# Slots of the late token tiles placed anew in a fused decoder step

## The reference

```python
def layer(x, c, ...):
    mod = jax.nn.silu(c) @ w_mod + b_mod
    sh1, sc1, g1, sh2, sc2, g2 = jnp.split(mod, N_MOD, axis=-1)
    m, st = token_mixers(modulate(x, sh1, sc1), w_in, ..., w_out, conv_buf, s0, past)
    x = x + g1[:, None, :] * m
    x = x + g2[:, None, :] * peer(modulate(x, sh2, sc2), peer_wq, peer_subkeys, peer_u, peer_v)
    return x, st
```

```python
    act = jax.nn.gelu(jnp.einsum('thkd,td->thk', pu[eidx], xb), approximate=False) * gate
    return jnp.einsum('thk,kd->td', act, pv[eidx])
```

## Time and profile before

| | us |
|---|---|
| median of three runs | 2171.68 (2168.19 to 2176.35) |
| the profiled execution | 2157.73 |
| its span | 2155.9 |
| TensorE busy | 1614.1 |
| VectorE busy | 1442.2 |
| GpSimd busy | 873.9 |
| ScalarE busy | 491.2 |

### The profile page before, as it was taken

The page is one execution under the profiler, slowest core; times in us unless marked ns, Lnnn a source line. Parts: engine busy times, 40 slices in busy tenths (PEclk is TensorE's granted clock), DMA queues, the critical chain, the costliest instruction groups (busy, mean ns, idle before and its releaser), DMA issues.

```text
span 2155.9 us, 25076 instructions
## 1 busy us (share of the span) xinstructions
PE 1614.1 (75%) x8048; PEld 856.8 (40%) x8048; DVE 1442.2 (67%) x3392; ACT 491.2 (23%) x1348; POOL 873.9 (41%) x646
## 2 busy tenths in 40 slices
PE   6999978878876766767576666667786777777776
PEld 4545547546663432343243233334322432221222
DVE  4246766555369976667998666799867668664754
ACT  2112213111132222223222122323212222221221
POOL 0286770312016643334564333456333334443442
PEclk9999999888988987898899889879898988898999
DMA  8487647977668999999899999989999999999996
GB/s 287 125 264 249 225 128 237 313 228 229 225 258 322 377 418 414 411 414 384 313 381 414 415 415 410 388 328 387 410 388 392 414 389 365 400 413 385 420 397 276
DMA packets 169989, 733.39 MB, mean 340 GB/s; under 512 B 17757, under 2 KB 18606, under 8 KB 103154
## 3 DMA queue, kind: packets, MB, share of 16 engines
q0 software_dynamic: 75024, 545.82, 63.1%
q1 hardware_dynamic: 94834, 185.96, 25.0%
HBM read 722.69 MB, written 9.12 MB: 339 GB/s over the span
## 4 chain that ended last, share of the span: by engine, by line
DMA 34%; PE 33%; DVE 18%; issue 5%; POOL 4%; SPq 3%; ACT 3%; DVEq 0%; ACTq 0%; POOLq 0%
PE bank L474 32%; DMA RING<-in_peer_uv,R 19%; DMA R<-in_peer_uv,R 11%; DVE RING L2078 6%; DVE R L2078 2%; SPq L2347 2%; ACT R L1330 2%; POOL RING L2327 2%; DMA R<-in_w_out 1%; SPq L2406 1%; DMA R<-h2s_d 1%; PE bank L481 1%; POOL R L2327 1%; DVE R L1881 1%; POOL R L2307 1%
## 5 line engine op out<-in xcount | busy, mean ns | idle before, releaser
L474 PE MATMUL bank<-RING,R 128*64 128x512 f32 (+2 forms) x1560 | 542.3, 695 | 287.6 <-ACT R L1330 276.3
L2327 POOL DMA_INDIRECT RING<-in_peer_uv,R x390 | 448.6, 1150 | 727.3 <-PE bank L474 595.8
L474 PE MATMUL bank<-R 128*128 128x128 f32 (+6 forms) x2216 | 408.8, 389 | 145.0 <-ACT R L1330 131.9
L2078 DVE SCALAR_TENSOR_TENSOR RING<-RING,MV 128x1024 f32<-128x1024 f32 x288 | 362.9, 1260 | 189.4 <-DMA RING<-in_peer_uv,R 182.2
L474 PEld LDWEIGHTS bank<-RING,R 128*64 128x64 f32 (+2 forms) x1560 | 165.7, 165 | 565.6 <-issue 549.3
L474 PEld LDWEIGHTS bank<-R 128*128 128x128 f32 (+3 forms) x2216 | 255.7, 187 | 321.2 <-issue 315.6
L1319 ACT ACTIVATE R<-R 128x2 f32<-128x2 f32 x256 | 52.1, 203 | 1099.8 <-DVE RING L2078 892.9
L2327 POOL DMA_INDIRECT R<-in_peer_uv,R x130 | 145.6, 1120 | 218.7 <-PE bank L474 200.5
L2078 DVE SCALAR_TENSOR_TENSOR R<-R,MV 128x1024 f32<-128x1024 f32 x96 | 126.4, 1316 | 82.9 <-DMA R<-in_peer_uv,R 82.1
L2078 DVE SCALAR_TENSOR_TENSOR RING<-RING,R 128x1024 f32<-128x1024 f32 x96 | 125.3, 1305 | 56.3 <-DMA RING<-in_peer_uv,R 51.9
L474 PEld LDWEIGHTS bank<-HT,R 128*128 128x128 f32 x1024 | 123.4, 196 | 47.0 <-issue 45.8
(11 more groups left out here) (320 smaller groups left out, 1765.4 us busy)
## 6 DMA issues: line engine op xcount, KB each, us to landing
R<-in_peer_wq SPq DMA_DIRECT2D x16, 2048.0 KB, 28.0
RING<-in_w_mod SPq DMA_DIRECT2D x12, 2048.0 KB, 8.1
MV<-in_cache_k SPq DMA_DIRECT2D x88, 256.0 KB, 3.8
R<-in_cache_v SPq DMA_DIRECT2D x84, 256.0 KB, 3.6
R<-in_w_out SPq DMA_DIRECT2D x6, 2048.0 KB, 32.9
MV<-in_cache_v SPq DMA_DIRECT2D x44, 256.0 KB, 3.7
RING<-in_w_in SPq DMA_DIRECT2D x5, 2048.0 KB, 9.5
R<-in_cache_k SPq DMA_DIRECT2D x40, 256.0 KB, 3.7
```

Of the source, the lines that this page charges most:

```text
L474: i = nc.tensor.matmul(out, lhsT, rhs, start=start, stop=stop, **k)
L2078: V.scalar_tensor_tensor(u, u, 1.0, H2HIGH if s_ % 2 and n < PAIRED * PH else H2[n // PH % 2], ALU.mult, ALU.mult, accum_out=DOT[:, n % 4, ...
L2327: nc.gpsimd.indirect_dma_start(UV[g % UN], None, a["peer_uv"][0], bass.IndirectOffsetOnAxis(ap=idx, axis=0)).then_inc(S(f"uv_in{g % UN}"), 16)
```

## The change

It changes at which event a slot stands. The order of the slots of a tile stays, and no instruction is added or removed.

```diff
-            slots = post_slots(tile)
-            at = max(len(delta_slots()), 112 - slots.index(("wq", 3, 0, 0)))
-            begin = delta_slots() if tile >= LATE else []
-            assert len(begin) <= at and at + len(slots) <= PH * STEPS
-            for first, some in ((0, begin), (at, slots)):
-                for x, s_ in enumerate(some):
-                    slots_at.setdefault((tile - 1) * PH * STEPS + first + x, []).append((tile,) + s_)
+            at = 0
+            for x, s_ in enumerate(delta_slots()):
+                at = x * 5 // 4 if tile < TILES - 1 else x
+                slots_at.setdefault((tile - 1) * PH * STEPS + at, []).append((tile,) + s_)
+            together = 0
+            for s_ in post_slots(tile):
+                together = together + 1 if s_[0] == "wq" else 0
+                at += together % 2 if together else 1
+                slots_at.setdefault((tile - 1) * PH * STEPS + at, []).append((tile,) + s_)
+            assert at < PH * STEPS
```

## The result

| | us |
|---|---|
| before, median of 20 runs | 2169.82 (2155.77 to 2180.34) |
| after, median of 20 runs | 2187.49 (2171.59 to 2208.26) |
| ratio, 95% interval | 1.0072 (1.0047 to 1.0098) |
| profiled execution after | 2175.94 |

The change makes the kernel slower by 0.7%. The medians lie 17.7 us apart; the ratio leaves out executions in a second, slower state of the chip, here the one of 2208.26 us. The forecast was 2171 us and no change, with 2187 as its upper end.

The account below looks back on a forecast made before the run. No engine alone bounds it; time can be won only where DMA runs under 415 GB/s. Terms - 7.0 + 6.0 + 0.5 = - 0.5 us gave 2157.2 profiled, 2171 us as median; range 2163 to 2180, with the terms' ends 2158 to 2187.

Parts of the forecast that it names:

- Two query slots to an event: Query slots behind value pairs: packing them wins nothing and costs 0.5 us in tile 3, ends 0 and 4.
- It fits: Four query slots behind a value pair take TensorE 6.0 us for two events, against 6.5 us the DMA needs.
- wq 2 and wq 3 0 to 3 us late, covered: Third and fourth query weights in tiles 1 and 2: 0 to 3 us late, covered by gathers taking 11.3 us to land.
- rival 1: Slower, 2190 us (+ 18 us): TensorE's waits for weights at slots 74 and 78, then wq 2 and 3; chance 0.19.
- The delta rule over 75 events: Tiles 1 and 2: spreading 60 delta slots relieves VectorE, 3.5 us gained per tile, together 7 us, ends 0 and 18.
- The output weights: w_out in tiles 1 and 2: later issue makes TensorE wait 4.4 then 9 us, costing 3 us per tile, ends 0 and 8.
- Rival 2: Delta units of VectorE: the relief works in full, 18 us won, 4 paid, - 14 us, 2157 us; chance 0.21.
- The tile's opening pile: Sums, residual, gate scaling, decays and products in the second tile's first delta unit: 9.6 of 12.8 us lost, stays.
- the signs of being wrong: Waits for wq over 5 us; pile shrunk over 2 us; a full-rate unit longer without weights moved into it.

Follow-up runs that it names:

- delta_only: Against the kernel before: delta rule over 75 events in tiles 1 and 2 as in the change, query slots still one to an event; 0.9989, 2163.39 us.
- after_spaced: The change with its query groups 10 events apart instead of 6; 1.0005 of the kernel before, 2173.05 us.
- pair_only: Against the kernel before: query slots two to an event in all three tiles, delta slots and first output slot left as before; 1.0102.
- pair_again: pair_only measured once more, word for word; 1.0085 of the kernel before.
- pair_beside: pair_only with seven eighths of each late query weight transfer sent to unread scratch, unwaited; 1.0019 of before, 1.0056 over the kernel before with the same split.
- the halved kernels: pair_beside and its base, the kernel before with the same split, each with half the late query matmuls left out; 1.0005 and 1.0017 of before.
- pair_act_late: pair_only with ScalarE's copy of each query block one event later; 1.0066 of the kernel before.
- tile3_old: The change with tile 3 left as before it; 1.0038 of the kernel before.

## Why the prediction was wrong, by its own steps

**Two query slots to an event: the step that failed.** It said "It fits" and counted 0.5 us, for tile 3 alone, with 4 as the upper end. Measured, the packing with its groups 6 events apart costs 1.0072 / 0.9989 against delta_only, 0.8% or 18 us, and 1.0072 / 1.0005 against after_spaced, 0.7% or 15 us; each has an interval of some 0.4% to each side. The duration was right (3.84 us for four slots). Two things were wrong:
- The steps were followed as if only w_out could hold TensorE for long, with "wq 2 and wq 3 0 to 3 us late, covered". In the trace there are five waits for `in_peer_wq`, 15.2 us together, up to 5.83. Behind the two of them that lasted 3.31 and 5.83 us in tiles 1 and 2, four slots took 5.23 and 5.68 instead of 3.84 us, at a granted clock of 0.72 over the first and of 0.50, the lower of the two levels, in the first 2 us of the second; behind two waits of under 1 us they took 3.84. Groups of 6 events at 3.25 us give 20 us, a transfer in the queue needs 23 or more. That arithmetic stood in rival 1 and should have been in the sum. In pair_only and pair_again the cover is used up in the unit of events 96 to 111, where the waits and the emptied queue stand together; in tiles 1 and 2 of the change's own profile the waits are there and the queue stays full.
- "Fits" compared TensorE's 6.0 us with 6.5 us for two events and left 0.5. The groups need more room than that: at 8 events to a group there is no wait for query weights and still 0.5% of loss, and pair_beside has 0.6% over its base without them. Which link in the loop of buffer, dot product, gelu, diagonal and value sum carries it is open. TensorE's own work is a candidate, but the halved kernels do not show it, as there the base slowed down and not the packed kernel sped up. ScalarE's in-order waits at the query copies (68.9 us against 22.6) are another; pair_act_late did not settle it.

**The delta rule over 75 events: 7 us of gain forecast, ends 0 and 18; none seen.** delta_only gives this and the w_out term together - 0.1%, - 2.4 us with an interval from - 8 to + 3; the forecast for the two was - 1. The sum agrees, but partly by luck: its two terms were not seen apart, and in the traces neither came out as forecast. In the traces the first two units win 2.1 us (18.6 to 16.5), less than the 4.0 forecast, while the third and fourth lose 6.7 more, not 0.5. The third unit was costed by VectorE's busy time staying under the floor (38.60 us it is, under 40.4), and it lost 5.1 us all the same. So busy time under the floor did not make a unit run at the floor where masks and corrections stand in it. And the fourth unit of before, with weights in flight, ran at 413 GB/s; with the delta tail moved in and the weights moved out it ran at 391, and in tile3_old, with the same slots, at 408. By this measure the four units together lose 4.6 us more than before and not 3.5 less; why delta_only is no slower for it is open.

**The output weights: 3 us a tile, ends 0 and 8.** The first wait came as forecast (4.4; 4.85 and 3.91 us in tiles 1 and 2). The second, 9 us, did not come: the longest w_out transfer took 41.3 us from issue to landing and held a weight load up for 0.8 us, where the longest of before took 50.4. The Trainium skill, "DMA: Bandwidth & Descriptors", section "Queues, rings and completion order", has the engines take turns between rings that have work; by it weights go faster as soon as TensorE's first wait thins out the gathers. The trace agrees, and that of before did so already: of tile 3's two transfers the first took 27.40 us and the median of both was 32.7, so the second some 38. In tiles 1 and 2 of before, where TensorE did not wait, the second took 50. I took 50, from there.

**Rivals.** Rival 1 (waits win, 2190, chance 0.19) had the sign and the size, 2190 against 2187. Its own condition, TensorE over 5 us at least three times a tile, was not met: in the trace two waits for weights last over 5 us in all, 5.83 and 7.82, and tile 3 had the like of the second before. Of its places, slots 74 and 78 cost nothing measurable, and how much wq 2 and 3 cost by their waits alone is not shown. So that it hit the number is in part luck. That the packed groups cost without waits stood in no rival. Rival 2 did not happen. The tile's opening pile moved by one event and lost 11.8 instead of 12.8 us, as said. Of the signs of being wrong two came: a wait for wq over 5 us, and a unit at full rate, the one at 1107, that got longer (40.8 to 45.4 us) without weights being moved into it.

## What to carry to other kernels

Where a ring of buffers keeps a DMA busy, look at how densely side work stands, and not only at its sum: compare the spacing of the slots that use double-buffered weights with a transfer's time under load, over all of them in a row, and not the first alone. Here groups of 6 events cost 0.7 to 1.0%, of 10 events nothing measurable, and at 8 events, about a transfer's time, some half of the loss was still there. Two slots in one event did no measurable harm as long as the groups kept their old distance. And before work is moved out of a stretch that another transfer keeps at full rate, look at the stretch that it goes to: here it ran slower there in the traces, though no timed run shows a cost.

## What was not expected of the hardware

In the unit at 1351 after the change no slots stand behind the value sums. TensorE waits 1.2 to 3.2 us before each of them, its granted clock is 0.67, and six of the nine value pairs take 3.13 to 3.68 us instead of 1.94. Before, the unit at 1343 still had slots, and 0.84. Ending the post slots ten events early did not free the last unit of a tile: it lost 3.9 us where the one before lost 2.4. That the low clock is the reason is not shown, as the same unit of tile3_old ran at 409 GB/s with a clock of 0.72.
